# A third seven-product step per w_ff2 group, and a row scale moved behind the product

## The reference

```python
h = rmsnorm(x, g_mlp[l])                      # x * rsqrt(mean(x*x) + eps) * g, per token
u = jnp.square(jax.nn.relu(jnp.einsum('bsd,df->bsf', h, w_ff1[l])))    # 2048 -> 8192
x = x + jnp.einsum('bsf,fd->bsd', u, w_ff2[l])                         # 8192 -> 2048
return rmsnorm(x, g_final)
```

## Time and profile before

| | us |
|---|---|
| median of 3 runs (lowest to highest) | 2383.79 (2383.69 to 2384.8) |
| profiled execution, its own time | 2383.24 |
| its span, first to last instruction | 2381.4 |
| PE busy | 2376.3 (100%) |
| DVE busy | 1700.8 (71%) |
| ACT busy | 1216.5 (51%) |

### The profile page before, as it was taken

One profiled execution on the slowest core, in us unless ns is written; L12 is line 12 of the kernel. 1 busy time (PEld: TensorE's weight loads), 2 busy tenths in 40 slices (PEclk: granted clock), 3 DMA queues, 4 the chain that ended last, 5 costly groups with the idle time before them and its releaser, 6 DMA issues.

```text
span 2381.4 us, 30785 instructions
## 1 busy us (share of the span) xinstructions
PE 2376.3 (100%) x12581; PEld 2034.9 (85%) x12581; DVE 1700.8 (71%) x1804; ACT 1216.5 (51%) x1427; POOL 0.2 (0%) x4
## 2 busy tenths in 40 slices
PE   9999999999999999999999999999999999999999
PEld 8888888888888888888888888888888888888887
DVE  6565666666568868868768667855778778886788
ACT  5444454554545445445445555555555455545554
POOL 0000000000000000000000000000000000000000
PEclk9999999999999999999999999999999999999999
DMA  7466556565555665655555554555555655565555
GB/s 253 160 188 197 166 186 196 192 188 195 186 186 178 220 215 189 213 181 200 200 191 192 182 186 159 171 183 185 186 180 195 198 190 175 185 219 186 189 173 180
DMA packets 238040, 452.15 MB, mean 190 GB/s; under 512 B 16569, under 2 KB 20779, under 8 KB 237771
## 3 DMA queue, kind: packets, MB, share of 16 engines
q1 hardware_dynamic: 237147, 449.07, 57.2%
q10 hardware_dynamic: 752, 1.12, 0.1%
HBM read 446.46 MB, written 3.67 MB: 189 GB/s over the span
## 4 chain that ended last, share of the span: by engine, by line
PE 97%; DVE 2%; ACT 0%; issue 0%; DMA 0%; ACTq 0%; DVEq 0%
PE PS L684 41%; PE PS L686 21%; PE PS L717 11%; PE PS L719 11%; PE PS L718 11%; DVE WL L1279 1%; PE PS L648 0%; PE PS L615 0%; PE PS L636 0%; PE PS L657 0%; ACT WH L840 0%; PE PS L625 0%; DVE PB L1259 0%; PE PS L553 0%; DMA VR<-in_g_mix 0%
## 5 line engine op out<-in xcount | busy, mean ns | idle before, releaser
L1279 DVE TENSOR_TENSOR WL<-RAW,WH 128x1024 fp32r<-128x1024 f32 (+1 forms) x844 | 1002.0, 1204 | 519.8 <-ACT WH L840 518.0
L684 PE MATMUL PS<-XHL,WH 128*128 128x512 f32 x3968 | 1248.9, 396 | 0.1
L840 ACT ACTIVATE WH<-RAW 128x1024 fp32r<-128x1024 f32 (+1 forms) x845 | 867.6, 1041 | 744.3 <-PE PS L686 478.2
L686 PEld LDWEIGHTS PS<-XHL,WL 128*128 128x128 f32 x3968 | 745.4, 188 | 176.0
L686 PE MATMUL PS<-XHL,WL 128*128 128x256 f32 x3968 | 779.8, 278 | 0.0
L684 PEld LDWEIGHTS PS<-XHL,WH 128*128 128x128 f32 x3968 | 605.2, 189 | 2.3 <-issue 1.3
L717 PE MATMUL PS<-WH,MHL 128*128 128x512 f32 x1000 | 390.2, 390 | 0.0
L719 PE MATMUL PS<-WH,MHL 128*128 128x512 f32 x1000 | 389.2, 389 | 0.0
L718 PE MATMUL PS<-WL,MHL 128*128 128x512 f32 x1000 | 389.1, 389 | 0.0
L719 PEld LDWEIGHTS PS<-WH,MHL 128*128 128x128 f32 x1000 | 187.7, 188 | 39.2
L718 PEld LDWEIGHTS PS<-WL,MHL 128*128 128x128 f32 x1000 | 187.8, 188 | 38.4
(11 more groups left out here) (212 smaller groups left out, 1373.2 us busy)
## 6 DMA issues: line engine op xcount, KB each, us to landing
RAW<-in_w_ff SPq DMA_DIRECT2D x256, 512.0 KB, 3.9
RAW<-in_w_in SPq DMA_DIRECT2D x224, 512.0 KB, 3.7
RAW<-in_w_up SPq DMA_DIRECT2D x176, 512.0 KB, 4.1
RAW<-in_w_down SPq DMA_DIRECT2D x88, 512.0 KB, 4.4
RAW<-in_w_mix_out SPq DMA_DIRECT2D x32, 512.0 KB, 3.9
RAW<-in_w_out SPq DMA_DIRECT2D x32, 512.0 KB, 3.5
RAW<-in_w_conv_out SPq DMA_DIRECT2D x16, 512.0 KB, 3.5
RAW<-in_w_attn_out SPq DMA_DIRECT2D x16, 512.0 KB, 4.1
```

Source lines behind the costliest of these rows:

```text
L684: mm(PS[:, b + p.banks[j], :], h[:, k, j * P:(j + 1) * P], x[:, kc, :], start=st, stop=False)
L686: t = mm(PS[:, b + p.banks[j], 0:T], l[:, k, j * P:(j + 1) * P], x[:, kc, 0:T], start=False, stop=en)
L840: act(high, raw, AF.Copy).then_inc(*own.made(hi, i))
L1279: tt(low, raw, high.bitcast(f32), sub).then_inc(*own.made(lo, i))
```

## The change

Groups of w_ff2 (name `ff`) do three pairs with seven products instead of two, and other ones: the second, fourth and sixth (`n` = 1, 3, 5) instead of the third and fifth (2, 4). The activation sums get three slots. `ff` items no longer scale by r2: ACT makes relu, the square into `MHL` and the square in place, and DVE adds each w_ff2 sum to the output with the factor r2 squared, a column of the token's partition, by scalar_tensor_tensor of 512 columns instead of tensor_tensor of 1024 where it reads PSUM. The spread of r2 over partitions (two small matmuls) goes. `EV` moves to the unused end of `PB` and `PT`.

```diff
-SEVEN = {"ff": (2, 4), "down8": (4, 5), "down6": (3,)}
+SEVEN = {"ff": ((1, 3, 5), (1, 3, 5)), "down8": ((4, 5), (4, 5)), "down6": ((3,), (3,))}
+PAIRS = {name: sorted(set(a) | set(b)) for name, (a, b) in SEVEN.items()}
...
-                if seg == 0 and g == 1:
-                    mid = {1: [("spread", "r2")]}
...
-            AXH = sb("AXH", [P, 2, 4, P], f32r, c=c)
+            AXH = sb("AXH", [P, 3, 4, P], f32r, c=c)
...
+        EV = [X[:].rearrange("p a b -> p (a b)")[:, 1024:1536] for X in (PB, PT)]
...
             def ff(it):          # ScalarE
                 yield from fold(it)
-                yield from nothing(2)
-                split_product(MHL, it.args["c0"], it.key, multiplied)
+                chain()
+                own.wait_ge(*left[it.key])
+                act(TA[:], TA[:], AF.Relu).then_inc(*own.made())
+                yield
+                chain()
+                act(MHL[:, it.args["c0"]:it.args["c0"] + 4, 0:T], TA[:], AF.Square).then_inc(*own.made())
+                chain()
+                act(TA[:], TA[:], AF.Square).then_inc(*own.made(part_hi, it.key))
                 free["TA"] = evacuated, it.key
...
+                if key == "r2":
+                    chain()
+                    tt(R2SQ, R[key], R[key], mul).then_inc(*own.made(column, "r2 squared"))
+                else:
+                    diagonals(key)
...
             def ff(it):          # VectorE
                 yield from fold(it)
-                scale_rows(scaled, it.key)
-                yield
-                chain()
-                stt(TA[:], TA[:], 0.0, TA[:], mx, mul).then_inc(*own.made(multiplied, it.key))
                 yield
                 split_product(MHL, it.args["c0"], it.key)
                 yield
                 yield from sums_x(it)
+
+            def squared_rows(x, product, tb):
+
+                chain()
+                return stt(x, product, R2SQ[:, tb:tb + 1], x, mul, add)
...
             def half_sums(it, half, key):
...
-                chain()
                 own.wait_ge(*used[it.steps[-1].ents[half]])
-                tt(x4, x4, PS[:, b:b + 2, :], add).then_inc(*own.made(evacuated, key))
+                if it.args["u"][0] == "ff":
+                    squared_rows(x4[:, 0, :], PS[:, b, :], 0).then_inc(*own.made())
+                    squared_rows(x4[:, 1, :], PS[:, b + 1, :], 1).then_inc(*own.made(evacuated, key))
...
             def sevens(it):
...
+                if rows2:
+                    squared_rows(x2, both, 1).then_inc(*own.made())
...
+                if rows2:
+                    squared_rows(xr[:, 0, :], PS[:, b + 3, :], 0).then_inc(*own.made())
+                    squared_rows(xr[:, 1, :], PS[:, b + 3, :], 1).then_inc(*own.made(left, it.key))
```

More of the change, by code:

```diff
@@ L159, in stream, with pairs @@
         return self.made[key]
-    def pairs(self, w, row0, kcs, col0, name):
+    def pairs(self, w, row0, kcs, g, name):
         steps = []
@@ L165, in pairs @@
             for half in range(2):
-                r, c = row0 + 2 * n * P, col0 + 512 * half
+                r, c = row0 + 2 * n * P, 1024 * g + 512 * half
                 self.units.append((w[r:r + 2 * P, c:c + 512].rearrange("(k p) n -> p k n", p=P), 2, 512))
-            seven, e = n in SEVEN[name], len(self.ents)
+            seven, e = n in SEVEN[name][g], len(self.ents)
             if seven:
@@ L172, in pairs @@
                 self.ents.extend(("unit", first + half) for half in range(2))
-            steps.append(Step(seven, list(range(e, len(self.ents))), kcs[2 * n:2 * n + 2]))
+            steps.append(Step(seven, list(range(e, len(self.ents))), kcs[2 * n:2 * n + 2],
+                              PAIRS[name].index(n) if seven else None))
         return steps
@@ L189, in group @@
     def group(self, kind, key, w, row0, kcs, g, name, src, **kw):
-        item = Item(kind, key, [], src, self.turn, steps=self.pairs(w, row0, kcs, 1024 * g, name), **kw)
+        item = Item(kind, key, [], src, self.turn, steps=self.pairs(w, row0, kcs, g, name), **kw)
         self.turn ^= 1
@@ L1037, in sums_x @@
                 u = it.args["u"]
-                for i, pair in enumerate(SEVEN[it.args["name"]]):
+                for i, pair in enumerate(PAIRS[it.args["name"]]):
                     if pair // 2 == it.args["c0"] // 4:
@@ L1063, in sevens @@
                 chain()
-                e.copy(EV[:, 0, :], PS[:, 4 * (it.side ^ 1), :]).then_inc(*own.made(pair1, it.key))
+                e.copy(EV[0], PS[:, 4 * (it.side ^ 1), :]).then_inc(*own.made(pair1, it.key))
                 free["EV"] = it.key
@@ L1623, in sevens @@
                 xr = XT[:, :, c + 512:c + 1024]
-                p1, p16 = EV[:, 0, :], EV[:, 1, :]
-                chain()
+                p1, p16 = EV
+                both = p1[:, None, :].to_broadcast([P, 2, 512])
+                rows2 = it.args["u"][0] == "ff"
                 own.wait_ge(*pair1[it.key])
-                tt(x11, x11, p1, add).then_inc(*own.made())
+                if rows2:
+                    squared_rows(x11, p1, 0).then_inc(*own.made())
+                else:
+                    chain()
+                    tt(x11, x11, p1, add).then_inc(*own.made())
                 chain()
@@ L1630, in sevens @@
                 yield
-                chain()
-                tt(x12, x12, p16, add).then_inc(*own.made())
+                if rows2:
+                    squared_rows(x12, p16, 0).then_inc(*own.made())
+                else:
+                    chain()
+                    tt(x12, x12, p16, add).then_inc(*own.made())
                 chain()
@@ L1635, in sevens @@
                 yield
[L1636 to L1640 removed]
+                if rows2:
+                    squared_rows(x2, both, 1).then_inc(*own.made())
+                else:
+                    chain()
+                    tt(x2, x2, both, add).then_inc(*own.made())
+                yield
+                if rows2:
+                    squared_rows(xr[:, 0, :], PS[:, b + 3, :], 0).then_inc(*own.made())
+                    squared_rows(xr[:, 1, :], PS[:, b + 3, :], 1).then_inc(*own.made(left, it.key))
+                else:
+                    chain()
+                    tt(xr, xr, PS[:, b + 3, None, :].to_broadcast([P, 2, 512]), add).then_inc(*own.made(left, it.key))
                 yield
```

29 lines of the change are left out of this document (14 added, 15 removed).

## The result

The changed kernel takes 2395.22 us (median of 4 runs, 2394.68 to 2396.36), the kernel before 2384.3 us beside it (4 runs, 2383.69 to 2385.12). The ratio is 1.0047, with a 95% interval of 1.0036 to 1.0059: slower by 10.9 us. The forecast was 2390.8, some 7 us slower. Its sign and its place hold, its size is 4 us short, and the result lies 1.2 us above the bounds of 2388 to 2394 that the forecast itself was given. The profiled execution took 2394.77 us with a span of 2393.0, so 11.6 us more span than before; what follows accounts for nearly all of these 11.6.

A forecast was written before the change was run, and what follows sets the result against it. PE's instructions laid end to end bound the kernel; -4.96 saved, +10.4 bank waits and +1.6 third-pair waits sum to +7.0 us, giving 2390.8 us; range 2380.5 to 2397.5, the forecast's own 2388 to 2394.

The forecast's parts named there:

- The mechanism: PE waits at second pair of three segments' second groups for the bank DVE's half sums free, 3.4 us each.
- ledger of an engine's queue: DVE's instructions timed in queue order through a segment's w_ff2 groups; half sums from 47.56, ending 50.64 us.
- less PE work (23 matmuls): Seven groups: one more seven-product step each, 4.76 us saved; with the spread of r2, -4.96 us together.
- the spread: Two small matmuls of 128 columns for r2 leave PE; from 0 to 0.56 us, taken as 0.2.
- third pair, four first groups: Third pair of each segment's first group: PE waits 0.4 us for a split on DVE; four segments, 1.6 us.
- second groups' banks, three times: Second group of three segments: PE waits 3.4 us for a bank at second pair; 10.2 and 0.2 more.
- granted clock: Forecast stays 1.00; rival: 1.2 GHz for one seven-product step behind each stall, 14 us, 2405 us; chance 0.07.
- waits on DVE of 1.3 us in all: Whole span before the change: PE's weight loads waited 1.1 us, matmuls 0.2; cited for the rival without waits.
- starving inside the groups: Rival: DVE also starves PE inside the groups, 1 us more in each of seven, 2397 us; chance 0.13.
- 3.4 us of backlog: First group's end: DVE begins evacuating the seven-product banks 3.4 us after PE ends the sixth pair; before, 2.6.
- rival of short waits: Rival: the bank wait is only 0.3 to 2 us a segment, smaller backlog; 2381 to 2386 us; chance 0.17.
- PE never waits: Rival: DVE keeps ahead throughout, no wait in the w_ff2 groups, 2378.8 us; chance 0.08.

## Why the prediction was right, and where it fell short

**The mechanism held, in its place.** PE waits at the second pair of three second groups for the half sums of the group before (line 1617). 23 matmuls are gone, as said (25 records). The half sums began 797.18 - 749.27 = 47.91 us after the first group's start, where the working had 47.56; the first part of the evacuation 783.71 - 749.27 = 34.44, where it had 34.36; the wait at the third pair was 0.5 against 0.4. A ledger of an engine's queue, made from increments of the timeline before, was good to 0.4 us over 48.

**The terms, forecast and measured:**

| term | forecast | measured |
|---|---|---|
| less PE work (23 matmuls) | -4.96 | 21 x 0.227 and 0.45 for the spread: -5.2 |
| third pair, four first groups | +1.6 | 4 x 0.52 = +2.1 |
| second groups' banks, three times | +10.4 | starts 0.9 + 0.9 + 0.7, second pairs 3 x 2.76: +10.8 |
| restart behind the long waits | 0 | 3 x 0.1 = +0.3 |
| granted clock | 0 | 1.6 + 1.3 = +2.9 |
| span | +7.0 | sum +10.9, read +11.6 |

Of the 0.7 left over, 0.3 lies ahead of the ff items (659.01 against 658.75), where nothing was changed, and most of the rest is rounding in the length of a group: 5.45 and 4.76 make 42.22 us before, and the trace has 42.17.

The spread was worth 0.45 us, not 0.2: rows 5 list 16 records and the changed kernel 12, so each matmul there leaves two records and the two that go are four records, not two, of 281 ns each. The wait of 3.4 us is rounded up too. From the ledger's own entries it is 50.64 - (41.93 + 5.45) = 3.26, which takes 0.4 us off the sum. And "waits on DVE of 1.3 us in all" leaves out one of 1.0 us for SQ in the same list; it comes once and lies outside these groups.

**The step that failed is the clock.** The prediction said that the granted clock would still be 1.00, and priced its fall as a rival at 0.07, with 14 us. It fell behind two of three long waits in the profiled run, to the lower level of 1.2 GHz, and cost 1.6 and 1.3 us. Without them the result would have been some 2392, inside the forecast's 2388 to 2394; that 2395.2 is still inside the whole range is owed to a rival, starving inside the groups, which reached to 2397 and did not happen. Both the chance and the price of the fall were off: it lasts eight slow matmuls, not a seven-product step for each of three stalls at half speed. No row of before could size it, for PE never waited there for long; the right conclusion from that was a wider bound on the forecast's own range, not a small chance. The kernel with zeros in the wait shows the clock's share apart from everything else, 2.9 us in the three groups and 3.1 in the span. The Trainium skill (TensorE: Matmul & The Clock Gate, Part 1) says that idleness throttles the array and activity releases it, and the traces agree in part: two of the three long waits at full idle are followed by 1.2 GHz and the third, as long, is not; the same waits filled with matmuls on zeros never are.

**A wait that I had computed and not seen.** In the prediction's own ledger the two instructions of 512 end at 41.84 + 0.75 = 42.6 us, and PE starts the second group at 41.9. Those instructions free the banks in which that group begins. I followed only the bank named for the second pair. The 0.9 us at the group's start was thus in the numbers; it hardly moved the sum, since PE, that much later, waits less at the second pair (3.64 together, against 3.26). The difference is the half sums, 3.18 us for four instead of the 3.07 worked out, and their start 0.35 later, less the 0.1 us that PE itself had lost by then.

**The backlog.** The prediction took the wait for 3.4 us of backlog in DVE's queue, and priced the rival of short waits by a smaller one. The kernel whose first groups have two steps has a smaller one, 2.7 us against 783.71 - 780.42 = 3.3 in the changed kernel, and waits just as long, for PE's own lateness shrinks with it. The wait can't be read from the backlog alone; it is the distance between two queues that both move. What shortens it is less work ahead of the half sums: 2.8 to 1.0 us with the split of t13 behind them, to nothing with the step put later.

**The rivals.** *PE never waits* (2378.8) is what the two kernels with the steps at the third, fourth and sixth pair came near, at 2381.9 and 2381.4. *DVE starves PE inside the groups* was not in the changed kernel: its third segment's second group takes 44.40 us, all of it pairs, the long wait and the restart. It did appear once two steps stood in a row, 0.25 to 0.46 us in a group. DVE's 71% is no measure for this, as the norm alone shows: 31 us off DVE, and no time.

**What stays open.** Why the clock falls behind some of the long waits and not behind others of the same length. In the profiled run of the changed kernel it was the first and second segment, in the one with two-step first groups the second and third, and in the one with the steps alone, whose waits are the shortest of the three, all. The means over whole runs (0.998 and 0.999 for the same kernel) fit a number of falls that varies, three stretches that lack 1.7 us each being 0.2% of the span; only the profiled runs show them one by one.

## What to carry to other kernels

When work is moved earlier in a tile, ask for each bank that it takes who gives it back, and where that instruction stands in its engine's queue; what decides is the order there, not the engine's share of busy time, and not even its backlog. Check both sides of a double buffer, since one instruction put ahead of an evacuation delays both. And price a wait on TensorE above its own length: here a wait that made PE 2.8 us late cost up to 4.5 (45.98 us for a group of 41.5), while waits of 1 us or less cost little more than themselves.

## What the runs showed of the hardware

- A wait of 2.0 to 2.6 us between the slot that was due and the next start (1.9 to 2.5 us idle in the list) can drop the granted clock to 1.2 GHz for the next eight matmuls or so: 0.43 us apart for 512 columns instead of 0.23, 1.3 to 1.6 us by the length of the group. It happened behind two of the three waits (2.4 to 2.5) in each of two profiled runs, and behind all three (1.9 each) of the kernel with the steps alone. After waits of up to 1.0 us the clock was 1.00 in every window read.
- The fall comes about when PE starts again, not when it stops. 798 to 800, with PE fully idle, still reads 1.00, and 800 to 802 reads 0.64 with PE's start at 800.41. In the second segment it came first: 978 to 980 reads 0.51, and PE starts at 978.51. In the kernel with the steps alone the clock is still 1.00 when PE starts (1154 to 1156 reads 0.96, PE starts at 1155.28) and reads 0.50 from 1156 on.
- Matmuls on zeros keep the clock up as well as real ones: 1.00 in all windows around 24 records over 2.84 us, in three groups, and a mean of 1.000 in all six runs.
- A stream restarted after a wait needs a moment: the first matmul takes 0.50 instead of 0.39 and its successor comes 0.34 later instead of 0.23, even at full clock (792.20 and 792.54). So a wait costs some 0.2 to 0.3 us more than its listed idle time: 0.5 for 0.34 listed, 0.9 for 0.64, 2.76 for 2.44.
- scalar_tensor_tensor with a column costs 751 ns at 512 elements and 1284 ns at 1024 where tensor_tensor takes 0.69 and 1.22 us: some 0.06 us more, whatever the size.
